# A tuned two-layer hybrid transformer trunk: the gated sum's halves in buffers of their own, copied one gate step behind each sum, and the second output tile's weights rounded earlier

## The chip, the cores and the metric

One core of one Trainium2 chip. The metric is the device time of one execution in microseconds; a kernel's time is the median of its runs. Durations of single instructions come from one further execution that was profiled.

## What is computed

The reference is a trunk of two layers over 512 latent and 256 context tokens of width 1024. Each layer normalises and modulates its input, projects it, and feeds three token mixers (grouped-query attention A, neighbourhood attention B, gated DeltaNet C). The change lies where the three are merged:

```python
def merge_branches(o_a, o_b, o_c, gate_raw, w_branch, w_out):
    br = jnp.einsum('btnc,ncd->btnd', jnp.stack([o_a, o_b, o_c], axis=-2), w_branch)
    gates = jax.nn.sigmoid(heads(gate_raw, N_BRANCH))
    return jnp.sum(gates * br, axis=-2) @ w_out
...
    x = x + gt_m * merge_branches(o_a, o_b, o_c, gate, w_branch, w_out)
    x = x + gt_f * sq_relu_mlp(modulate(rms_norm(x, norm_ffn), sh_f, sc_f), w_ffn1, w_ffn2)
```

All of it is float32. Layer 0 works on 768 tokens (context and latent), layer 1 from here on only on the 512 latent ones.

## The kernel before

Activations are kept transposed: partitions are channels, a *slice* `k` is 128 of the 1024 channels by all tokens. Each projection multiplies in three passes to keep float32 accuracy: the weights and the activations are each split into a high part, rounded to the type `fp32r`, and a low part, the rest. `project` (L452) adds high x high, high x low and low x high (L461, L462, L463) over the eight slices, and the 768 tokens go in two runs of 496 and 272 columns. `project_abreast` (L466) does the same for several output tiles, five slices of all tiles first, then the other slices tile by tile, with a wait (`ready`) for each slice, so that it can begin before all slices are there; its matmuls are L475, L476, L477.

The weights come tile by tile in one fixed order (`order`). SP brings a tile into one of three places of `wring`; ACT rounds it into `wh` (`high`, L1135, one of three places, free when TensorE has finished the tile three before); POOL subtracts and writes `wl` (`split`, L1903). TensorE waits for POOL's part (`weights`). `high(l, name, i)` rounds up to two tiles beyond the one named, `ahead=0` only as far as that one. Each engine's instructions stand in program order, and an engine that waits holds all that stands behind.

The stage around the change, for each layer:

- TensorE computes, for x = 0 to 23, the gate tile x (from the normalised input, halves `hh` and `hl`) and the branch tile x (from a branch's halves `ohi`, `olo`). x runs over branch C, then A, then B, with eight output slices each. Then the eight output tiles follow, 0 and 1 abreast, from the halves of the gated sum.
- ACT takes the sigmoid of gate tile x (L1368). DVE multiplies it with branch tile x (L1808) and, from x = 8, adds it to the sum `mT` (L1811). The sum's slice k is complete at x = 16 + k.
- The sum's halves go into `hh` (ACT, L1375) and `hl` (DVE, L1796), the buffers from which the gate projections read. So they wait for gate projection 23. ACT copies the eight slices there, and only behind them rounds the weights of output tiles 1 and 2. On DVE the first subtraction stands before the last multiplication, the other seven behind the last addition.
- Behind the output tiles ACT squares the new residual for the norm (L1072), TensorE sums the squares, and ACT and DVE make the new `hh` and `hl`.

`R` is one buffer of 27648 words for each partition that the stages share: the branch outputs and their halves, the sum `mT` at 9216 (`S0`), the sigmoids `gsig` at 15360, the norm's squares `sq_n`, root `rs_n` and products `ht`, and the feed-forward temporaries `ftmp`.

Of the kernel before, what the change touches and what calls it, by code (L numbers as in the profile page):

```python
# [15 lines left out]
F32 = mybir.dt.float32  # L16
F32R = mybir.dt.float32r
ALU = mybir.AluOpType
ACT = mybir.ActivationFunctionType
AX = mybir.AxisListType  # L20

P = 128
D = 1024
KC = D // P
LAT, CTX = 512, 256
TOK = LAT + CTX
# [16 lines left out]
GF = 4  # L43
# [65 lines left out]
def program(nc, a, out, x_store, skew, bias_rows, z_store, book):  # L109
    book["final"] = book.get("final", False)  # L110
    with ExitStack() as ctx:
# [28 lines left out]
        hh, hl = (ctx.enter_context(nc.sbuf_tensor(n, [P, KC, TOK], F32R)) for n in ("hh", "hl"))  # L140
# [9 lines left out]
        r_at = nc.sbuf_base if not callable(nc.sbuf_base) else nc.sbuf_base()  # L150
        r_at = (r_at + 31) // 32 * 32
# [11 lines left out]
        def r(at, *shape):  # L163
            n = int(np.prod(shape))
            v = R[:, at:at + n]
            if len(shape) == 2:
                v = v.rearrange("p (a b) -> p a b", a=shape[0])
            if len(shape) == 3:
                v = v.rearrange("p (a b c) -> p a b c", a=shape[0], b=shape[1])
            return v  # L170
# [2 lines left out]
        oC, oA, oB = r(0, 4, TOK), r(3072, 4, TOK), r(6144, 4, TOK)  # L173
        S0 = 9216

        N0 = 4 * GF * TOK
        sq_n, rs_n, ht = r(N0, 2, TOK), r(N0 + 2 * TOK, TOK), r(N0 + 3 * TOK, 3, TOK)
        ftmp = r(N0, 2, TOK)
        xT = r(XT0, KC, TOK)
        fin_T = nc.alloc_sbuf_tensor_at("fin_T", [P, KC, LAT], F32, offset=h_at)  # L180

# [31 lines left out]
        eraw = r(S0 + 3072, 2, 8, 32)  # L213

        mT = r(S0, KC, TOK)
        gsig = r(S0 + 6144, 2, TOK)
        prow = sb("prow", [P, P])
        mrow = sb("mrow", [P, P])
# [48 lines left out]
        act_done, dve_done, pool_done, pe_done = sig("act_done"), sig("dve_done"), sig("pool_done"), sig("pe_done")  # L267
# [14 lines left out]
        def full(*key):  # L282
            n = book.get(("ps",) + key, 0) if book["final"] else 0
            return ps_full[n % 4], n // 4 + 1
# [36 lines left out]
        def att_pairs(l):  # L321

            return [(br, hp, t) for br in "AB" for hp in range(A_H // 2) for t in range(TT if l == 0 else LT)]
# [109 lines left out]
        def weights(pe, l, name, i=0):  # L433

            pe.wait_ge(*pool_done.at("wlo", l, name, i))
            s = where[l, name, i][2] % NSPL
            return slot_view(wh, s, l, name, i), slot_view(wl, s, l, name, i)
# [10 lines left out]
        def _(pe):  # L448
            turn["n"] = 0
            mm, tr = nc.tensor.matmul, nc.tensor.transpose  # L450

            def project(key, w, ntok, rhs=None, kn=KC, m0=0, ready=None, ps=None, done=True):  # L452

                (ah, al), (rh, rl) = w, rhs or (hh, hl)
                ps = take(pe, *key)[:, landing(ntok):landing(ntok) + ntok]
                for t0, t1 in runs(ntok):
                    for k in range(kn):
                        if ready and t0 == 0:
                            pe.wait_ge(*ready(k))
                        ahk, alk = ah[:, k, m0:m0 + P], al[:, k, m0:m0 + P]  # L460
                        mm(ps[:, t0:t1], ahk, rh[:, k, t0:t1], start=(k == 0), stop=False)  # L461
                        mm(ps[:, t0:t1], ahk, rl[:, k, t0:t1], start=False, stop=False)  # L462
                        last = mm(ps[:, t0:t1], alk, rh[:, k, t0:t1], start=False, stop=(k == kn - 1))  # L463
                last.then_inc(*filled(*key))

            def project_abreast(jobs, ntok, ready):  # L466

                homes = [take(pe, *key)[:, landing(ntok):landing(ntok) + ntok] for key, _ in jobs]

                def products(i, k):  # L470

                    key, (ah, al) = jobs[i]
                    for t0, t1 in runs(ntok):
                        to = homes[i][:, t0:t1]
                        mm(to, ah[:, k, :], hh[:, k, t0:t1], start=(k == 0), stop=False)  # L475
                        mm(to, ah[:, k, :], hl[:, k, t0:t1], start=False, stop=False)  # L476
                        last = mm(to, al[:, k, :], hh[:, k, t0:t1], start=False, stop=(k == KC - 1))  # L477
                    return last

                for k in range(ABREAST):  # L480
                    pe.wait_ge(*ready(k))
                    for i in range(len(jobs)):
                        products(i, k)
                for i, (key, _) in enumerate(jobs):
                    for k in range(ABREAST, KC):
                        if i == 0:
                            pe.wait_ge(*ready(k))
                        last = products(i, k)
                    last.then_inc(*filled(*key))
# [199 lines left out]
            for l in range(DEPTH):  # L689
                if l == 0:  # L690

                    for t in range(TT):
                        pe.wait_ge(*x_in[t].at())
                        ps = take(pe, "x", t)
                        for k in range(KC):
                            last = tr(ps[:, k * P:k * P + P], r(S0 + 1024 * t, 1024)[:, k * P:k * P + P], ident)
                        last.then_inc(*filled("x", t))
                if l == 0:
# [8 lines left out]
                    for t in range(TT):  # L707
                        last = mm(ps[:, t * P:t * P + P], small[:, 16 + t:17 + t].to_broadcast([P, P]), ident,
                                  start=True, stop=True)
# [15 lines left out]
                for p in range(2, 15):  # L725
# [9 lines left out]
                    if p == 2:  # L735
                        pe.wait_ge(*read("baT", l))
                        ps = take(pe, "ba", l)
                        for t in range(TT):
                            last = tr(ps[:, 16 * t:16 * t + 16], baT[0:16, t * P:t * P + P], ident[0:16, 0:16])
                        last.then_inc(*filled("ba", l))  # L740
                    if p == 6:
# [7 lines left out]
                        for c in range(2):  # L749
                            last = mm(sums[:, :, 16 + 8 * c:24 + 8 * c], blk[:, 64 * c:64 * c + 1].to_broadcast([P, P]),  # L750
                                      gt[:, :, :], start=True, stop=True)
# [21 lines left out]
                for s in range(TT):  # L773
                    turned = None
                    for i in range(5):
                        for d in range(2):
# [3 lines left out]
                            last = halves(ps, srcT, src)  # L780
                            if i < 4:
                                last = halves(ps[:, 512:768], src, srcT)
# [16 lines left out]
                    for d in range(2):  # L799
# [3 lines left out]
                        for h in range(C_H):  # L803
                            for c, lo in enumerate((0, HALF)):
                                c0 = 512 * c + h * HALF
                                last = mm(ps[:, c0:c0 + HALF], kbuf[d][lo:lo + HALF, h, :], xbuf[d][lo:lo + HALF, h, :],  # L806
                                          start=True, stop=True)
# [5 lines left out]
                    for c in range(2):  # L813
                        n = 2 * s + c
# [8 lines left out]
                        for h in range(C_H):  # L823
                            for d in range(2):
                                mm(new[d][:, h * P:h * P + P], xbuf[d][rows[d], h, :], vbbuf[d][rows[d], h, :],
                                   start=(h == 0), stop=False)
# [4 lines left out]
                        for h in range(C_H):  # L831
                            for d in range(2):
                                ins = mm(new[d][:, h * P:h * P + P], cdbuf[d][:, chunk[d], h, :], S[:, 4 * d + h, :],
                                         start=False, stop=(h == C_H - 1))
# [3 lines left out]
                        o = [so[d][rows[d], 512:1024] for d in range(2)]  # L838
                        if out_wanted:
# [3 lines left out]
                            for h in range(C_H):  # L843
                                for d in range(2):
                                    mm(o[d][:, h * P:h * P + P], qdbuf[s % 2][d][:, chunk[d], h, :], S[:, 4 * d + h, :],
                                       start=(h == 0), stop=False)
# [60 lines left out]
                for x in range(24):  # L907
# [4 lines left out]
                            ready=(lambda k: dve_done.at("olo", l, n, k)) if x % 8 == 0 else None)  # L912
                    slot_read(l, "br", x, "br", l, x)
                project_abreast([(("out", l, i), weights(pe, l, "out", i)) for i in range(2)], nt,
                                lambda k: dve_done.at("mlo", l, k))
                for i in range(8):
                    if i >= 2:
                        project(("out", l, i), weights(pe, l, "out", i), nt)
                    slot_read(l, "out", i, "out", l, i)

                if l == DEPTH - 1:
# [142 lines left out]
        def _(act):  # L1064
            A = nc.scalar.activation
# [87 lines left out]
            for l in range(DEPTH):  # L1153
# [202 lines left out]
                def branch_high(l, n, k):  # L1356

                    A(ohi[n][:, k, 0:nt], (oA, oB, oC)[n][:, k, 0:nt], ACT.Copy).then_inc(*act_done.mark("ohi", l, n, k))

                act.wait_ge(*dve_done.at("o", l, len(att_pairs(l)) - 1))  # L1360
                for k in range(4):
                    branch_high(l, 2, k)
                for x in range(24):
# [4 lines left out]
                    A(gsig[:, x % 2, 0:nt], landed(nt, "gate", l, x), ACT.Sigmoid).then_inc(*free("gate", l, x))  # L1368
                    if 1 <= x < 9:
                        branch_high(l, (x - 1) // 4, (x - 1) % 4)  # L1370
                for k in range(KC):

                    act.wait_ge(*full("gate", l, 23))
                    act.wait_ge(*dve_done.at("merge", l, 16 + k))
                    A(hh[:, k, 0:nt], mT[:, k, 0:nt], ACT.Copy).then_inc(*act_done.mark("mhi", l, k))  # L1375
                for i in range(8):
                    high(l, "out", i)
                    if i == 0:
# [43 lines left out]
        def _(dve):  # L1422
# [128 lines left out]
            for l in range(DEPTH):  # L1551
# [241 lines left out]
                def merged_low(l, k):  # L1793

                    dve.wait_ge(*act_done.at("mhi", l, k))
                    V.tensor_tensor(hl[:, k, 0:nt], mT[:, k, 0:nt], hh[:, k, 0:nt].bitcast(F32), ALU.subtract)\  # L1796
                        .then_inc(*dve_done.mark("mlo", l, k))

                for x in range(24):
                    n, dc = divmod(x, 8)  # L1800
                    if x == 23:

                        dve.wait_ge(*full("gate", l, 23))
                        merged_low(l, 0)
                    dve.wait_ge(*full("br", l, x))
                    dve.wait_ge(*read("gate", l, x))
                    g, acc = gsig[:, x % 2, 0:nt], mT[:, dc, 0:nt]
                    V.tensor_tensor(g if n else acc, landed(nt, "br", l, x), g, ALU.mult).then_inc(*free("br", l, x))  # L1808
                    dve.wait_ge(*read("br", l, x))
                    if n:  # L1810
                        V.tensor_tensor(acc, acc, g, ALU.add).then_inc(*dve_done.mark("merge", l, x))  # L1811
                    else:
                        V.memset(small[:, 63:64], 0.0).then_inc(*dve_done.mark("merge", l, x))
                    if 1 <= x < 9:
                        branch_low(l, (x - 1) // 4, (x - 1) % 4)
                for k in range(1, KC):
                    merged_low(l, k)

                def residual(key, j, gate):

# [325 lines left out]
```

## Time and profile before

| | us |
|---|---|
| median of 3 runs | 3033.19 |
| lowest, highest | 3032.58, 3040.96 |
| the profiled execution, its own time | 3049.55 |
| its span | 3047.8 |
| TensorE matmuls busy (PE) | 2868.9 (94%) |
| TensorE weight loads busy (PEld) | 2456.4 (81%) |
| DVE busy | 1182.2 (39%) |
| ACT busy | 1034.4 (34%) |
| POOL busy | 1032.9 (34%) |
| granted TensorE clock, mean | 0.982 |

Busy times are sums over an engine's instructions in the one profiled execution; PE and PEld are the same engine, whose weight loads run beside its matmuls. Matmuls are pipelined: one is listed with 0.39 us, and the next starts 0.22 us later. The stage of the change is at 1155 to 1186 us in layer 0 and at 2622 to 2645 us in layer 1.

### The profile page before, as it was taken

The page shows a single profiled execution, that of the slowest core. Times are in us where ns is not written, and L with a number is a line of the kernel's source. Part 1 is how long each engine was busy: PE and PEld are TensorE (multiplying, and loading weights), DVE is VectorE, ACT ScalarE, POOL GpSimd, SP SyncE. Part 2 cuts the span into 40 slices and gives each one's busy share as a digit, 9 for nine tenths or more (in the row PEclk, how much of TensorE's full clock was granted, in tenths as well). Part 3 has the DMA queues.
Part 4 walks back from the last instruction along what each step waited for, and adds up shares of the span by engine and source line. Part 5 has one row for each costly group of instructions (what it writes and reads, how often), then busy time and mean ns, then how long its engine had stood idle before and what let it go on. Part 6 is the DMA issues. An engine that isn't in the chain of part 4 may idle for free. (4 is left out here: it accounts for less than half of the span.)

```text
span 3047.8 us, 57451 instructions
## 1 busy us (share of the span) xinstructions
PE 2868.9 (94%) x24823; PEld 2456.4 (81%) x24823; DVE 1182.2 (39%) x1813; ACT 1034.4 (34%) x1763; POOL 1032.9 (34%) x697
## 2 busy tenths in 40 slices
PE   6998899998999999999999999899999999999999
PEld 5887788876688888788888878788786788778887
DVE  3754443245631113422222267555235711242223
ACT  3542222225532112422222245433226532342223
POOL 3334434220323333222222223355430344434443
PEclk8999999999999999999999999999999999999999
DMA  7226344110012232122222122100320034323332
GB/s 252 63 67 214 136 150 132 42 42 1 12 42 64 64 108 63 49 63 63 64 69 63 63 83 63 43 3 3 90 56 2 15 100 135 95 83 96 97 101 80
DMA packets 306028, 230.89 MB, mean 76 GB/s; under 512 B 25265, under 2 KB 277617, under 8 KB 304881
## 3 DMA queue, kind: packets, MB, share of 16 engines
q1 hardware_dynamic: 299152, 202.48, 22.1%
q0 software_dynamic: 3776, 17.91, 1.6%
q10 hardware_dynamic: 2848, 6.82, 0.6%
q8 instruction: 198, 3.24, 0.4%
q14 instruction: 54, 0.43, 0.0%
HBM read 216.17 MB, written 11.98 MB: 75 GB/s over the span
## 5 line engine op out<-in xcount | busy, mean ns | idle before, releaser
L1903 POOL TENSOR_TENSOR wl<-wring,wh 128x1024 fp32r<-128x1024 f32 (+1 forms) x310 | 721.3, 2328 | 1358.7 <-ACT wh L1135 1354.3
L461 PE MATMUL ps<-hh,wh 128*128 128x496 f32 (+2 forms) x2312 | 822.8, 356 | 6.5 <-DVE R L1754 3.5
L463 PE MATMUL ps<-hh,wl 128*128 128x496 f32 (+2 forms) x2312 | 811.4, 351 | 0.0
L462 PE MATMUL ps<-hl,wh 128*128 128x496 f32 (+2 forms) x2312 | 811.1, 351 | 0.0
L461 PEld LDWEIGHTS ps<-hh,wh 128*128 128x128 f32 x2312 | 436.4, 189 | 69.5 <-issue 6.6
L462 PEld LDWEIGHTS ps<-hl,wh 128*128 128x128 f32 x2312 | 436.8, 189 | 57.3 <-issue 3.6
L463 PEld LDWEIGHTS ps<-hh,wl 128*128 128x128 f32 x2312 | 436.2, 189 | 54.6
L1135 ACT ACTIVATE wh<-wring 128x1024 fp32r<-128x1024 f32 (+1 forms) x310 | 305.7, 987 | 498.6 <-PE ps L463 458.9
L1824 DVE SCALAR_TENSOR_TENSOR R<-ps,modcs,R 128x512 f32<-128x512 f32 x216 | 136.3, 659 | 362.6 <-PE ps L463 339.8
L461 PE MATMUL ps<-fh,wh 128*128 128x496 f32 (+2 forms) x768 | 272.6, 355 | 0.0
L463 PE MATMUL ps<-fh,wl 128*128 128x496 f32 (+2 forms) x768 | 272.0, 354 | 0.0
L462 PE MATMUL ps<-fl,wh 128*128 128x496 f32 (+2 forms) x768 | 271.6, 354 | 0.0
L617 PE MATMUL ps<-R 64*64 64x64 f32 x5376 | 181.9, 221 | 27.9 <-issue 8.5
L617 PEld LDWEIGHTS ps<-R 64*64 64x64 f32 x5376 | 167.6, 136 | 44.2 <-issue 22.7
L1843 DVE TENSOR_TENSOR R<-R 128x768 f32<-128x768 f32 (+1 forms) x64 | 66.1, 1032 | 341.1 <-ACT R L1392 341.1
L1808 DVE TENSOR_TENSOR R<-ps,R 128x768 f32<-128x768 f32 (+1 forms) x48 | 39.6, 824 | 392.7 <-PE ps L463 392.7
L462 PEld LDWEIGHTS ps<-fl,wh 128*128 128x128 f32 x768 | 144.7, 188 | 19.0
L463 PEld LDWEIGHTS ps<-fh,wl 128*128 128x128 f32 x768 | 144.4, 188 | 19.4
L461 PEld LDWEIGHTS ps<-fh,wh 128*128 128x128 f32 x768 | 144.4, 188 | 19.2
L990 ACT ACTIVATE R<-ps,stat 128x768 f32<-128x768 f32 (+2 forms) x160 | 116.4, 730 | 119.6 <-DVE stat L1496 117.1
L1496 DVE TENSOR_REDUCE stat<-ps 128x1 f32<-128x768 f32 (+2 forms) x160 | 114.5, 741 | 38.0 <-PE ps L571 35.8
L1392 ACT ACTIVATE R<-ps 128x768 f32<-128x768 f32 (+1 forms) x64 | 45.1, 705 | 235.7 <-PE ps L463 174.2
(257 smaller groups left out, 3873.8 us busy)
## 6 DMA issues: line engine op xcount, KB each, us to landing
wring<-in_w_ffn SPq DMA_DIRECT2D x128, 512.0 KB, 3.6
wring<-in_w_in SPq DMA_DIRECT2D x110, 512.0 KB, 3.6
wboth<-in_w_mod SPq DMA_DIRECT2D x80, 512.0 KB, 6.3
wring<-in_w_branch SPq DMA_DIRECT2D x32, 256.0 KB, 2.7
wring<-in_w_out SPq DMA_DIRECT2D x16, 512.0 KB, 4.1
x_store<-R POOLq DMA_DIRECT2D x2, 3072.0 KB, 9.9
R<-x_store POOLq DMA_DIRECT2D x2, 3072.0 KB, 10.9
wring<-in_w_in SPq DMA_DIRECT2D x16, 256.0 KB, 3.4
```

The costliest lines, as they stand in the source:

```text
L461: mm(ps[:, t0:t1], ahk, rh[:, k, t0:t1], start=(k == 0), stop=False)
L462: mm(ps[:, t0:t1], ahk, rl[:, k, t0:t1], start=False, stop=False)
L463: last = mm(ps[:, t0:t1], alk, rh[:, k, t0:t1], start=False, stop=(k == kn - 1))
L617: last = mm(out[lo:lo + HALF, h * HALF:h * HALF + HALF], left[lo:lo + HALF, h, :], right[lo:lo + HALF, h, :], start=True, stop=True)
L990: nc.scalar.activation(prob[br][p % 2][:, u, 0:n], score_ps(l, p)[u][:, 0:n], ACT.Exp, bias=stat[:, sl, 0:1], accum_out=stat[:, sl, 1:2])\
L1135: A(slot_view(wh, n % NSPL, *slot), w, ACT.Copy).then_inc(*act_done.mark("whi", *slot))
L1392: A(f, landed(nt, "ff1", l, j), ACT.Relu).then_inc(*free("ff1", l, j))
L1496: V.tensor_reduce(stat[:, sl, 0:1], ps[:, 0:n], AX.X, ALU.max, negate=True)\
L1808: V.tensor_tensor(g if n else acc, landed(nt, "br", l, x), g, ALU.mult).then_inc(*free("br", l, x))
L1824: V.scalar_tensor_tensor(out=xT[:, j, t0:t1], in0=landed(nt, *key)[:, t0:t1], scalar=modc[:, gate + j, c:c + 1], in1=xT[:, j, t0:t1], op0= ...
L1843: V.tensor_tensor(f, f, f, ALU.mult).then_inc(*dve_done.mark("fsq", l, j))
L1903: G.tensor_tensor(slot_view(wl, n % NSPL, l, name, i), w, slot_view(wh, n % NSPL, l, name, i).bitcast(F32), ALU.subtract)\
```

## The change

1. The gated sum's halves are `mh`, at word 0 of `R` (over the branch buffers that are used up by then), and `ml`, in the place of `mT` itself. Output projections read them (`rhs=(mh, ml)`).
2. ACT copies slice k at gate step x = 17 + k, behind that step's sigmoid, and slice 7 behind the loop; the wait for gate projection 23 is gone. DVE subtracts slice k at the start of step 17 + k, before that step's multiplication, and slice 7 behind the loop.
3. At x = 23 ACT rounds output tile 1's weights directly behind the sigmoid, before it copies slices 6 and 7.
4. Since `ml` now stays in use during the output projections, the norm's squares, root and products get other places in `R` (`rs_n` at 15360, `sq_n` at 16896, `ht` behind it); `ftmp` stays at 12288.

```diff
-        N0 = 4 * GF * TOK
-        sq_n, rs_n, ht = r(N0, 2, TOK), r(N0 + 2 * TOK, TOK), r(N0 + 3 * TOK, 3, TOK)
-        ftmp = r(N0, 2, TOK)
+        N0 = 16896
+        rs_n, sq_n, ht = r(15360, TOK), r(N0, 2, TOK), r(N0 + 2 * TOK, 3, TOK)
+        ftmp = r(4 * GF * TOK, 2, TOK)
...
+        mh, ml = (nc.alloc_sbuf_tensor_at(n, [P, KC, TOK], F32R, offset=r_at + 4 * o) for n, o in (("mh", 0), ("ml", S0)))
...
-            def project_abreast(jobs, ntok, ready):
+            def project_abreast(jobs, ntok, ready, rhs=None):
+
+                rh, rl = rhs or (hh, hl)
...
                 project_abreast([(("out", l, i), weights(pe, l, "out", i)) for i in range(2)], nt,
-                                lambda k: dve_done.at("mlo", l, k))
+                                lambda k: dve_done.at("mlo", l, k), rhs=(mh, ml))
                 for i in range(8):
                     if i >= 2:
-                        project(("out", l, i), weights(pe, l, "out", i), nt)
+                        project(("out", l, i), weights(pe, l, "out", i), nt, rhs=(mh, ml))
...
+                def merged_high(l, k):
+
+                    act.wait_ge(*dve_done.at("merge", l, 16 + k))
+                    A(mh[:, k, 0:nt], mT[:, k, 0:nt], ACT.Copy).then_inc(*act_done.mark("mhi", l, k))
...
-                for k in range(KC):
-
-                    act.wait_ge(*full("gate", l, 23))
-                    act.wait_ge(*dve_done.at("merge", l, 16 + k))
-                    A(hh[:, k, 0:nt], mT[:, k, 0:nt], ACT.Copy).then_inc(*act_done.mark("mhi", l, k))
+                    if x == 23:
+                        high(l, "out", 1, ahead=0)
+                    if x >= 17:
+                        merged_high(l, x - 17)
+                merged_high(l, KC - 1)
...
-                    V.tensor_tensor(hl[:, k, 0:nt], mT[:, k, 0:nt], hh[:, k, 0:nt].bitcast(F32), ALU.subtract)\
+                    V.tensor_tensor(ml[:, k, 0:nt], mT[:, k, 0:nt], mh[:, k, 0:nt].bitcast(F32), ALU.subtract)\
...
-                    if x == 23:
-
-                        dve.wait_ge(*full("gate", l, 23))
-                        merged_low(l, 0)
+                    if x >= 17:
+                        merged_low(l, x - 17)
...
-                for k in range(1, KC):
-                    merged_low(l, k)
+                merged_low(l, KC - 1)
```

The order of ACT's instructions from the sigmoid of step 22 to the rounding of output tile 2, layer 0, before (`wh` is rounded weights, 128x512 a branch tile's, 128x1024 the others'; the square of the new residual follows later):

```order
L1368 ACTIVATE R<-ps 128x768
L1135 ACTIVATE wh<-wring 128x512
L1135 ACTIVATE wh<-wring 128x1024
L1368 ACTIVATE R<-ps 128x768
L1375 ACTIVATE hh<-R 128x768 x8
L1135 ACTIVATE wh<-wring 128x1024 x2
L1077 ACT_TABLE_LOAD
```

and in the changed kernel:

```order
L1377 ACTIVATE R<-ps 128x768
L1367 ACTIVATE mh<-R 128x768
L1139 ACTIVATE wh<-wring 128x512
L1139 ACTIVATE wh<-wring 128x1024
L1377 ACTIVATE R<-ps 128x768
L1139 ACTIVATE wh<-wring 128x1024
L1367 ACTIVATE mh<-R 128x768 x2
L1139 ACTIVATE wh<-wring 128x1024
L1081 ACT_TABLE_LOAD
```

Each list begins with the sigmoid of step 22. Tile 1's weights now stand directly behind the sigmoid of step 23 and before the last two copies; the other six copies are spread over the steps before.

DVE's instructions over steps 22 and 23 and the last halves, layer 0, before:

```order
L1808 TENSOR_TENSOR R<-ps,R 128x768
L1811 TENSOR_TENSOR R<-R 128x768
L1796 TENSOR_TENSOR hl<-R,hh 128x768
L1808 TENSOR_TENSOR R<-ps,R 128x768
L1811 TENSOR_TENSOR R<-R 128x768
L1796 TENSOR_TENSOR hl<-R,hh 128x768 x7
```

and in the changed kernel:

```order
L1805 TENSOR_TENSOR ml<-R,mh 128x768
L1815 TENSOR_TENSOR R<-ps,R 128x768
L1818 TENSOR_TENSOR R<-R 128x768
L1805 TENSOR_TENSOR ml<-R,mh 128x768
L1815 TENSOR_TENSOR R<-ps,R 128x768
L1818 TENSOR_TENSOR R<-R 128x768
L1805 TENSOR_TENSOR ml<-R,mh 128x768
```

One subtraction now precedes each multiplication, and one instead of seven stands behind the last addition.

## Rows read from the trace of the kernel before

**Rows 1.** The page, part 1: busy us, share of the span, instructions.
```profile
PE 2868.9 (94%) x24823; PEld 2456.4 (81%) x24823; DVE 1182.2 (39%) x1813; ACT 1034.4 (34%) x1763; POOL 1032.9 (34%) x697
```

**Rows 2.** Timeline, layer 0: start, us, engine, line, operation, count [idle before <-releaser].
```profile
1155.24 0.81 ACT L1368 ACTIVATE R<-ps 128x768 f32<-128x768 f32 x1 [7.26 <-PE ps L463]
1155.95 5.23 ACT L1375 ACTIVATE hh<-R 128x768 fp32r<-128x768 f32 x7
...
1159.05 0.29 PE L463 MATMUL ps<-ohi,wl 128*128 128x272 f32 x1
...
1160.43 0.96 DVE L1811 TENSOR_TENSOR R<-R 128x768 f32<-128x768 f32 x1
...
1162.23 1.99 ACT L1135 ACTIVATE wh<-wring 128x1024 fp32r<-128x1024 f32 x2
...
1163.41 2.78 POOL L1903 TENSOR_TENSOR wl<-wring,wh 128x1024 fp32r<-128x1024 f32 x1 [12.28 <-ACT wh L1135]
...
1166.29 0.75 PE L475 MATMUL ps<-hh,wh 128*128 128x496 f32 x1 [6.95 <-POOL wl L1903]
```

**Rows 3.** Timeline, layer 1.
```profile
2622.16 0.60 ACT L1368 ACTIVATE R<-ps 128x512 f32<-128x512 f32 x1 [4.37 <-PE ps L463]
...
2622.65 4.37 ACT L1375 ACTIVATE hh<-R 128x512 fp32r<-128x512 f32 x8
...
2624.40 0.39 PE L463 MATMUL ps<-ohi,wl 128*128 128x512 f32 x1
...
2626.93 1.99 ACT L1135 ACTIVATE wh<-wring 128x1024 fp32r<-128x1024 f32 x2
...
2628.11 2.80 POOL L1903 TENSOR_TENSOR wl<-wring,wh 128x1024 fp32r<-128x1024 f32 x1 [7.71 <-ACT wh L1135]
...
2631.01 0.76 PE L475 MATMUL ps<-hh,wh 128*128 128x512 f32 x1 [6.22 <-POOL wl L1903]
```

**Rows 4.** Timeline: one slice apart near the end of tile 1, both layers.
```profile
1184.91 0.39 PE L475 MATMUL ps<-hh,wh 128*128 128x496 f32 x1
...
1185.97 0.39 PE L461 MATMUL ps<-hh,wh 128*128 128x496 f32 x1
...
2643.92 0.39 PE L475 MATMUL ps<-hh,wh 128*128 128x512 f32 x1
...
2644.60 0.39 PE L461 MATMUL ps<-hh,wh 128*128 128x512 f32 x1
```

**Rows 5.** Timeline of POOL and DVE; last, the subtraction's min/median/max ns.
```profile
1147.90 0.96 DVE L1811 TENSOR_TENSOR R<-R 128x768 f32<-128x768 f32 x1
1148.12 3.00 POOL L1903 TENSOR_TENSOR wl<-wring,wh 128x1024 fp32r<-128x1024 f32 x1 [2.63 <-ACT wh L1135]
...
1184.26 2.41 POOL L1903 TENSOR_TENSOR wl<-wring,wh 128x1024 fp32r<-128x1024 f32 x1 [15.02 <-ACT wh L1135]
...
2617.93 2.47 POOL L1903 TENSOR_TENSOR wl<-wring,wh 128x1024 fp32r<-128x1024 f32 x1 [1.39 <-ACT wh L1135]
...
L1796 DVE TENSOR_TENSOR hl<-R,hh x16: 678/948/3129, 1156.9 to 2634.2; 128x768 fp32r<-128x768 f32 x8, 128x512 fp32r<-128x512 f32 x8
```

**Rows 6.** Timeline: TensorE's starts after two shorter idle times.
```profile
334.15 1.04 PE L617 MATMUL ps<-R 64*64 64x64 f32 x29 [2.03 <-issue]
...
700.91 1.87 PE L571 MATMUL ps<-R 64*128 64x512 f32 x4 [1.57 <-ACT R L990]
```

**Rows 7.** Windows: A:B us, busy of PE, PEld, DVE, ACT, POOL; granted clock, DMA, GB/s.
```profile
334.20:338.00 3.80, 3.75 (x114) 3.42 (x117) 1.77 (x5) 0.77 (x2) 0.00 (x0) 1.00 0.90 336
...
700.90:704.60 3.70, 3.69 (x18) 2.03 (x20) 1.54 (x4) 0.41 (x2) 0.00 (x0) 0.54 0.00 0
...
1240.50:1250.70 10.20, 6.39 (x22) 5.31 (x23) 8.06 (x14) 6.32 (x10) 0.82 (x1) 0.50 0.19 53
...
2631.00:2636.40 5.40, 5.39 (x13) 4.24 (x14) 3.84 (x3) 0.00 (x0) 2.69 (x1) 0.50 0.60 175
...
2680.90:2687.70 6.80, 3.99 (x15) 3.15 (x16) 5.22 (x9) 3.71 (x6) 1.46 (x1) 0.50 0.27 77
```

More of the change, by code:

```diff
@@ L474, in products @@
                         to = homes[i][:, t0:t1]
-                        mm(to, ah[:, k, :], hh[:, k, t0:t1], start=(k == 0), stop=False)
-                        mm(to, ah[:, k, :], hl[:, k, t0:t1], start=False, stop=False)
-                        last = mm(to, al[:, k, :], hh[:, k, t0:t1], start=False, stop=(k == KC - 1))
+                        mm(to, ah[:, k, :], rh[:, k, t0:t1], start=(k == 0), stop=False)
+                        mm(to, ah[:, k, :], rl[:, k, t0:t1], start=False, stop=False)
+                        last = mm(to, al[:, k, :], rh[:, k, t0:t1], start=False, stop=(k == KC - 1))
                     return last
```

## The prediction, made blind

> **What bounds the kernel now.** I read the page first. TensorE is busy for 2868.9 us, 94% of the span [rows 1], so work that is shifted on the other engines pays only where TensorE stands still for it. The change touches one place in each of the two layers, so the second view is the timeline around the step from the last branch projection to the first output tiles. In layer 0 the last branch matmul starts at 1159.05 and ends at 1159.34; the next one starts at 1166.29 after 6.95 us of idle time, released by POOL's low half of the weights [rows 2]. In layer 1 the end is 2624.79 (2624.40 and 0.39), the next start 2631.01, the idle time 6.22 us, the releaser the same [rows 3]. Those 13.17 us are what is there to be had directly.
>
> Follow the chain back in layer 0. Output tiles 0 and 1 are computed abreast, so TensorE waits for the weights of both. POOL splits the weights of tile 1 from 1163.41, because ACT rounded them at 1162.23, because ACT first copied eight slices of the gated sum: seven from 1155.95 to 1161.18, and the eighth behind the last addition, which DVE ended at 1161.39. ACT had been free for something else since the sigmoid of 1155.24. Layer 1 reads the same: eight copies from 2622.65, the rounding at 2626.93, POOL at 2628.11.
>
> A third view, the windows, gives the second cost. TensorE's granted clock is 0.50 (1.2 GHz, half of 2.4) from 2631.00 to 2636.40, while the matmuls start again [rows 7]; in layer 0 it is likewise. Its price is read from start to start. At full clock one slice of one tile takes 1.06 us in layer 0 (1184.91 to 1185.97) and 0.68 us in layer 1 (2643.92 to 2644.60) [rows 4]; 16 of them are 16.88 us (16 x 1.055, the second decimal being rounded in the rows) and 10.88 us. They took 1185.97 - 1166.29 = 19.68 us and 2644.60 - 2631.01 = 13.59 us. The low clock after the idle time costs 2.80 + 2.71 = 5.51 us.
>
> **The change part by part.**
>
> *The high halves move.* Eight ACT copies per layer no longer write the buffer that the gate projections read, so they need not wait for gate projection 23. Slice k is copied at gate step 17 + k, behind the sigmoid; the eighth stays at the end. Nothing is added: the same eight copies, of some 0.75 us (5.23 / 7) in layer 0 and 0.55 us (4.37 / 8) in layer 1. What is queued behind a copy on ACT are the roundings for the next branch and gate tiles. Their lows are ready early: the one that TensorE needs at the end of layer 1's branch 23 (2624.79) is done at 2617.93 + 2.47 = 2620.40 [rows 5], 4.4 us before; in layer 0 it is 1151.12 for 1159.34, 8.2 us before. That cover pays for a copy, so I cost it at nothing.
>
> *The low halves move.* Eight DVE subtractions (0.95 and 0.68 us, [rows 5]) go ahead of the multiplication of the same step. DVE waits there for the copy, some 1.6 us after a gate projection ends, while the branch result comes 4.1 us after it in layer 0 (1155.24 to 1159.34) and 2.6 in layer 1. 1.6 + 0.95 and 1.2 + 0.68 fit. Nothing, again.
>
> *Tile 1's weights are rounded ahead.* The rounding now sits directly behind the last sigmoid, where the first copy started: 1155.95 and 2622.65. From ACT's start to POOL's start it was 1162.23 to 1163.41 and 2626.93 to 2628.11, 1.18 to 1.20 us both times. POOL therefore starts at about 1157.15 and 2623.84. The length of POOL's instruction is the one open term. The same shape took 2.78 and 2.80 us in these two places, 2.41 us at 1184.26, 2.47 us at 2617.93, and 3.00 us at 1148.12, where DVE's addition (1147.90 to 1148.86) was under way when it started [rows 5]. At 1157.15 and 2623.84 no DVE instruction is under way, so I take 2.41 and 2.45, with 3.00 as the other end. The low half of slice 6 on DVE then starts while POOL works. Subtractions beside POOL took up to 3.129 us where the median was 0.948 [rows 5]; it is stretched to about POOL's end, and pushes the last multiplication, addition, copy and subtraction by 1 to 2 us. The last of them, low half 7, is then ready at about 1164.5 and 2630, and TensorE asks for it only after ten abreast products and two more (12 x 1.055 and 12 x 0.68 us): at 1172.3 and 2634.5. This is hidden.
>
> Here the Trainium skill has a rule that speaks against the edit. The page "SBUF — State Buffer", section "SBUF: two separate sides", says that GpSimd and a VectorE instruction with two SBUF inputs share a port pair as an exclusive lock, so that the one which starts first holds it and the other blocks. If a subtraction got in first, POOL would stand for up to a whole subtraction, and the sum below would be smaller by up to 0.95 + 0.68 us. By the order of starts above POOL is first, and then the rule and my sum agree.
>
> TensorE's first matmul came 0.10 us after POOL's end both times (1163.41 + 2.78 to 1166.29, 2628.11 + 2.80 to 2631.01). The new starts are 1157.15 + 2.41 + 0.1 = 1159.66 and 2623.84 + 2.45 + 0.1 = 2626.39. Gained: 1166.29 - 1159.66 = 6.63 us and 2631.01 - 2626.39 = 4.62 us, together 11.25. Idle time of 0.3 and 1.6 us is left; the weights of tile 1 are late still, and they remain the releaser.
>
> *The clock.* After 2.03 us of idle time before 334.15 the granted clock stayed at 1.00; after 1.57 us before 700.91 it was 0.54 [rows 6, 7]. With 0.3 us in layer 0 I expect no fall; with 1.6 us in layer 1 either is possible. Matmuls run without a break on both sides of it, so I take no fall, and 5.51 us come back whole. A fall would cost at most the old 2.71.
>
> *The homes of the norm's squares, roots and products move.* No instruction, shape or wait changes with them; zero, and the first use of the new places is behind the last read of the old contents. No row of the trace shows an address costing time: the branch halves in the same buffer and the halves in the old one both give matmuls of 0.39 us.
>
> **Sum.** 11.25 + 5.51 = 16.8 us. Against the profiled execution's 3049.55 that is 3032.8. The median of the runs shown is 3033.19, 16.36 us below that execution; none of the terms depends on the difference, so I subtract there too: **3016.4 us**, 0.55% faster. Changes within 0.3% (9.1 us) could hardly be told from none here; the runs shown lie 8.4 us apart.
>
> **Rivals.**
>
> *A, the forecast.* Both gaps nearly close and the clock holds: 3016.4. Bounds of its terms: both POOL instructions at 3.00 us give 3017.5; no idle time left at all gives 3014.5. Chance 0.68.
>
> *B, the clock falls in layer 1 after all.* 2.7 us come back as loss, with POOL's 1.1 us: 3020.2. For it: 0.54 after 1.57 us. Against it: 1.00 after 2.03 us. Chance 0.14.
>
> *C, the gain is given back in later clock stretches.* Everything behind 1160 moves, and how long the clock stays low after a stall differs between like stalls. The norm of layer 0 had 10.2 us at 0.50 and the same norm in layer 1 6.8 us [rows 7]; the 3.4 us between them cost 1.7 us of work. Some ten stalls follow the first saved place; if five of them get a longer stretch, 8.5 us go: 3024.9, which is no longer to be told from no change. Against it: as many should get shorter. Chance 0.15.
>
> *D, slower.* The halves in the gate steps hold up the weights of the next tiles, in 14 steps (17 to 23, two layers). Price: each step adds its copy and subtraction to TensorE's path, 7 x (0.75 + 0.95) + 7 x (0.55 + 0.68) = 20.5 us, and the clock drops each time for 3.4 us, 14 x 1.7 = 23.8 us. 3016.4 + 44.3 = 3060.7. It decides from the point where the lows of a next tile come over 4.4 us later than now in layer 1, or 8.2 in layer 0. A copy and a locked subtraction beside it together are 3.7 us at most. Chance 0.03.
>
> **How the numbers follow.** The likeliest case gives 3016.4. A, B and C set the range: on the lower side A's 3014.5 less two or three clock stretches of luck, 3010; on the upper side up to just beyond C's middle, 3026. Over 9.1 us faster (below 3024.1): A, B and half of C, 0.88 rounded; within: the rest of C, 0.09; slower by over 9.1 us: D, 0.03.
>
> **What would show it.** Right: in the timeline the rounding of tile 1's weights directly behind the last sigmoid; POOL's split of 2.4 us; TensorE's idle time before the first output product at 0.3 and 1.6 us instead of 6.95 and 6.22, with the same releaser; granted clock 1.00 there; no idle time of TensorE in gate steps 17 to 23; one slow low half beside POOL. Wrong: another releaser (a low half, the copy of slice 7) before the first or the thirteenth product; a clock of 0.50 behind 2626; idle time before a gate or branch product; or a span that falls by much less than these two places gained, with longer stretches at 0.50 elsewhere.

## The result and the profile after

| | median, us | lowest to highest | runs |
|---|---|---|---|
| before, measured beside the change | 3037.19 | 3032.58 to 3044.78 | 6 |
| the change | 3022.05 | 3013.66 to 3027.44 | 6 |

The ratio is 0.9946, with a 95% interval of 0.9928 to 0.9965: 16.4 us less, between 10.6 and 21.9. (The ratio is worked out from all the runs and is not the quotient of the two medians, which lie 15.1 us apart.) Measured again beside the experiments, with another eight runs of the changed kernel, it was 0.9959 (0.9941 to 0.9978), 12.5 us less. The forecast was 16.8 us, 0.55%. One execution of an experiment below, of the kernel with the early rounding alone, took 10638.85 us at a granted clock of 0.481, and its ratio leaves it out.

The page of the changed kernel, its header and the line of part 1:

```profile
span 3020.4 us, 57433 instructions
...
PE 2855.1 (95%) x24823; PEld 2451.2 (81%) x24823; DVE 1180.0 (39%) x1813; ACT 1033.6 (34%) x1763; POOL 1032.0 (34%) x697
```

The instruction counts are those of before [rows 1], and the busy times of DVE, ACT and POOL agree with it within 2.2 us. The timeline of layer 0, for comparison with [rows 2] (this execution is 2.04 us ahead of the other at this place, for reasons that lie before it):

```profile
1153.20 0.81 ACT L1377 ACTIVATE R<-ps 128x768 f32<-128x768 f32 x1 [7.26 <-PE ps L465]
1153.91 1.05 ACT L1139 ACTIVATE wh<-wring 128x1024 fp32r<-128x1024 f32 x1
1154.86 0.84 ACT L1367 ACTIVATE mh<-R 128x768 fp32r<-128x768 f32 x1
1155.10 2.39 POOL L1909 TENSOR_TENSOR wl<-wring,wh 128x1024 fp32r<-128x1024 f32 x1 [6.02 <-ACT wh L1139]
1155.72 2.58 DVE L1805 TENSOR_TENSOR ml<-R,mh 128x768 fp32r<-128x768 f32 x1 [8.91 <-ACT mh L1367]
...
1157.01 0.29 PE L465 MATMUL ps<-ohi,wl 128*128 128x272 f32 x1
1157.59 0.46 PE L479 MATMUL ps<-mh,wh 128*128 128x496 f32 x1 [0.30 <-POOL wl L1909]
...
1159.21 0.96 DVE L1818 TENSOR_TENSOR R<-R 128x768 f32<-128x768 f32 x1
1160.20 0.85 ACT L1367 ACTIVATE mh<-R 128x768 fp32r<-128x768 f32 x1 [4.51 <-DVE R L1818]
...
1161.08 0.96 DVE L1805 TENSOR_TENSOR ml<-R,mh 128x768 fp32r<-128x768 f32 x1 [0.91 <-ACT mh L1367]
```

and of layer 1, for [rows 3]:

```profile
2601.93 1.05 ACT L1139 ACTIVATE wh<-wring 128x1024 fp32r<-128x1024 f32 x1
2602.88 0.62 ACT L1367 ACTIVATE mh<-R 128x512 fp32r<-128x512 f32 x1
2603.12 2.36 POOL L1909 TENSOR_TENSOR wl<-wring,wh 128x1024 fp32r<-128x1024 f32 x1 [3.44 <-ACT wh L1139]
2603.53 2.50 DVE L1805 TENSOR_TENSOR ml<-R,mh 128x512 fp32r<-128x512 f32 x1 [6.11 <-ACT mh L1367]
...
2605.58 0.47 PE L479 MATMUL ps<-mh,wh 128*128 128x512 f32 x1 [1.51 <-POOL wl L1909]
```

The rounding (L1139) stands directly behind the sigmoid (L1377), POOL's split (L1909) takes 2.39 and 2.36 us, and TensorE's idle time is 0.30 and 1.51 us with POOL's weights as its releaser still. The low half of slice 6 (L1805), which starts while POOL works, is stretched to 2.58 and 2.50 us; the last low half is done at 1162.04, and nothing on TensorE waits for it.

The windows of the changed kernel, first the gate steps 17 to 23 of both layers up to the last branch matmul (in layer 0 from 5.5 us behind the start of step 17), then the abreast products (columns as in [rows 7]):

```profile
1075.00:1157.20 82.20, 82.20 (x481) 73.92 (x479) 18.71 (x19) 21.27 (x27) 29.19 (x14) 1.00 0.33 106
2545.00:2603.90 58.90, 58.90 (x261) 48.59 (x259) 15.21 (x21) 19.75 (x29) 28.08 (x16) 1.00 0.49 156
...
1157.30:1172.00 14.70, 14.41 (x81) 12.86 (x82) 4.08 (x5) 3.58 (x5) 2.59 (x2) 1.00 0.25 72
2605.20:2616.00 10.80, 10.42 (x46) 8.69 (x47) 3.57 (x5) 4.30 (x6) 2.71 (x3) 1.00 0.33 99
```

TensorE is busy for the whole of the gate steps, and its trace shows no idle time before any matmul of them, so the halves cost nothing there. The granted clock behind the two places is 1.00. Before, it was 0.50 in layer 1 [rows 7] and likewise in layer 0:

```profile
1166.30:1172.10 5.80, 5.80 (x18) 5.09 (x19) 5.49 (x4) 0.00 (x0) 2.94 (x1) 0.50 0.57 167
```

**A measure that does not depend on the rest of the execution.** From the start of the last branch matmul to the start of output tile 2's first matmul the work is the same in every kernel here. Before, it ran from 1159.05 to 1185.97 and from 2624.40 to 2644.60 [rows 2 to 4]: 26.92 + 20.20 = 47.12 us. In the changed kernel it runs from 1157.01 to 1174.62 and from 2603.68 to 2616.55: 17.61 + 12.87 = 30.48 us. The two places give 16.64 us. Below, this sum is *the two places*.

The spans differ by more, 3047.8 - 3020.4 = 27.4 us. Of the other 10.8 us, 2.04 had come before 900 us, where both kernels do the same, and 6.6 us came in layer 0's feed-forward stage, which the last section takes up. The rest, some 2 us, is 0.3 us between the first place and that stage and 2.5 us between it and the second place, less 0.7 us lost behind the second place; the last section shows that such stretches differ from execution to execution.

### The profile page after: what moved, and what is told of

Read it like the earlier page. It is cut to its first block and busy times, and to the rows that moved or that the text cites. A ratio compares the mean times of both kernels' runs of the same rounds, so it can differ in the third digit from the quotient of the medians.

```text
span 3020.4 us, 57433 instructions
## 1 busy us (share of the span) xinstructions
PE 2855.1 (95%) x24823; PEld 2451.2 (81%) x24823; DVE 1180.0 (39%) x1813; ACT 1033.6 (34%) x1763; POOL 1032.0 (34%) x697
## 5 line engine op out<-in xcount | busy, mean ns | idle before, releaser
L1909 POOL TENSOR_TENSOR wl<-wring,wh 128x1024 fp32r<-128x1024 f32 (+1 forms) x310 | 720.7, 2326 | 1334.7 <-ACT wh L1139 1330.2
L463 PE MATMUL ps<-hh,wh 128*128 128x496 f32 (+2 forms) x2168 | 770.1, 355 | 6.5 <-DVE R L1763 3.5
L465 PE MATMUL ps<-hh,wl 128*128 128x496 f32 (+2 forms) x2168 | 759.5, 350 | 0.0
L464 PE MATMUL ps<-hl,wh 128*128 128x496 f32 (+2 forms) x2168 | 759.3, 350 | 0.0
L1139 ACT ACTIVATE wh<-wring 128x1024 fp32r<-128x1024 f32 (+1 forms) x310 | 305.8, 987 | 470.6 <-PE ps L465 448.1
L463 PEld LDWEIGHTS ps<-hh,wh 128*128 128x128 f32 x2168 | 408.9, 189 | 65.0 <-issue 6.6
L464 PEld LDWEIGHTS ps<-hl,wh 128*128 128x128 f32 x2168 | 409.3, 189 | 53.0 <-issue 3.4
L465 PEld LDWEIGHTS ps<-hh,wl 128*128 128x128 f32 x2168 | 408.8, 189 | 50.2
```

The costliest lines, as they stand in the source:

```text
L1139: A(slot_view(wh, n % NSPL, *slot), w, ACT.Copy).then_inc(*act_done.mark("whi", *slot))
L1909: G.tensor_tensor(slot_view(wl, n % NSPL, l, name, i), w, slot_view(wh, n % NSPL, l, name, i).bitcast(F32), ALU.subtract)\
```

## The experiments

Times are medians; each ratio is against runs of the kernel before on the same chip. The kernel before had 3043.35 us beside the first four kernels below, and 3041.17 us beside the other four.

### The early rounding alone

To the kernel before:

```diff
                     if 1 <= x < 9:
                         branch_high(l, (x - 1) // 4, (x - 1) % 4)
+                    if x == 23:
+                        high(l, "out", 1, ahead=0)
                 for k in range(KC):
```

> The kernel before, with one edit: output tile 1's weights are rounded directly behind the sigmoid of step 23; the halves stay in the old buffers and at their old places. My theory: both parts are needed, and this one alone closes most of layer 0's gap and part of layer 1's. POOL's split then starts at about 1157.2 and 2623.8 as in the changed kernel, but the low halves come late: the first one is stretched beside POOL, the second stands behind the last multiplication and addition. Idle time of TensorE from the last branch matmul to the fourth slice: about 1.8 us in layer 0 (6.95 before), about 4 us in layer 1 (6.22 before), in pieces before several slices, with DVE's low half as the releaser of the later pieces. Time: 10 to 13 us less than before. The rival, that the weights are all there is to it (the halves' new home is ornament): 16 to 17 us less, idle time 0.1 and 1.5 us. The other rival, that the halves set the start: 1 us less or none.

Measured: 3033.9 us, ratio 0.9967 (0.9951 to 0.9982), 10.0 us less. The two places: 19.07 (1152.48 to 1171.56) + 14.00 us = 33.07 us, 14.05 less than before. The timeline of this kernel, layer 0, then the two starts of layer 1:

```profile
1149.44 1.05 ACT L1135 ACTIVATE wh<-wring 128x1024 fp32r<-128x1024 f32 x1
1150.39 5.24 ACT L1377 ACTIVATE hh<-R 128x768 fp32r<-128x768 f32 x7
1150.64 2.39 POOL L1905 TENSOR_TENSOR wl<-wring,wh 128x1024 fp32r<-128x1024 f32 x1 [5.93 <-ACT wh L1135]
1151.33 2.52 DVE L1798 TENSOR_TENSOR hl<-R,hh 128x768 fp32r<-128x768 f32 x1 [8.88 <-ACT hh L1377]
...
1153.99 0.46 PE L475 MATMUL ps<-hh,wh 128*128 128x496 f32 x1 [1.22 <-DVE hl L1798]
...
1156.63 0.49 PE L475 MATMUL ps<-hh,wh 128*128 128x496 f32 x1 [0.29 <-DVE hl L1798]
...
2603.66 0.47 PE L475 MATMUL ps<-hh,wh 128*128 128x512 f32 x1 [2.13 <-DVE hl L1798]
2605.50 0.50 PE L475 MATMUL ps<-hh,wh 128*128 128x512 f32 x1 [0.21 <-DVE hl L1798]
```

The releaser changed, as expected: TensorE now waits for the first low half, which is held up beside POOL, and shortly for the second. But these waits are 1.5 and 2.3 us, not 1.8 and about 4. In layer 1 I had reckoned with one more locked subtraction in the way of slices 2 and 3. The trace has POOL's next split only at 2606.67, 1.17 us behind the start of the second slice, and no idle time of TensorE behind it. One line gives 84% of what the whole change gives at the two places.

### The halves' move alone

From the changed kernel:

```diff
-                    if x == 23:
-                        high(l, "out", 1, ahead=0)
```

> The changed kernel without the early rounding of output tile 1's weights: the halves have their own home and are made one step behind each sum, the weights are rounded where they were, behind the copy of slice 7. My theory: next to nothing. The copy of slice 7 waits for the last addition, the rounding comes behind it at its old time, POOL starts at its old time and only takes 2.4 instead of 2.8 us: idle time 6.6 and 5.8 us, low clock afterwards as before, time 1 us less than before. The rival, that the eight copies were the cause: 10 us or more less.

Measured: 3038.85 us, ratio 0.9989 (0.9973 to 1.0005), which can't be told from 1. The two places: 24.98 + 19.85 = 44.83 us, 2.29 less. The timeline of this kernel:

```profile
1160.38 0.96 DVE L1816 TENSOR_TENSOR R<-R 128x768 f32<-128x768 f32 x1
1161.37 0.84 ACT L1367 ACTIVATE mh<-R 128x768 fp32r<-128x768 f32 x1 [4.63 <-DVE R L1816]
1162.12 1.99 ACT L1139 ACTIVATE wh<-wring 128x1024 fp32r<-128x1024 f32 x2
...
1163.30 4.67 POOL L1907 TENSOR_TENSOR wl<-wring,wh 128x1024 fp32r<-128x1024 f32 x2 [12.22 <-ACT wh L1139]
...
1165.74 0.75 PE L479 MATMUL ps<-mh,wh 128*128 128x496 f32 x1 [6.45 <-POOL wl L1907]
...
2623.67 0.77 PE L479 MATMUL ps<-mh,wh 128*128 128x512 f32 x1 [5.71 <-POOL wl L1907]
```

Seven of eight copies were gone from the way, and the rounding started when it had before: the eighth copy waits for the last addition, and the rounding stands behind it. What is won is 0.50 and 0.51 us of idle time, since DVE is no longer in POOL's way (two splits in 4.67 us instead of 5.83 and 5.58), and some 1.4 us by a shorter low clock in layer 0, which only this one profile shows. The parts nearly add up: 14.05 and 2.29 us for 16.64. The halves' move is worth 2.3 us by itself, and 2.6 us behind the early rounding.

### The new places of the norm's data alone

The kernel before with only the lines on `N0`, `rs_n`, `sq_n`, `ht` and `ftmp` changed.

> The kernel before with only the norm's squares, root and products in their new places. My theory: no change (within 2 us), idle times 6.95 and 6.22 us as before. In the profiles of the two kernels layer 0's feed-forward stage had a pace of 220 ns from one 496-column matmul to the next in the changed kernel and 221 to 227 ns before, some 6.5 us over the stage. If the new places were the reason (the rival), this kernel's feed-forward stage has 220 ns and the time is 5 to 7 us less than before; if it is a matter of the single execution, the pace of this profile is one or the other and the time is unchanged.

Measured: 3041.73 us, ratio 0.9993 (0.9979 to 1.0008). Idle times 6.95 and 6.22 us, the two places 47.08 us: no change. Its profile did have the faster pace of the feed-forward stage, and yet its median stands with the kernel before, so the new places are not what makes the stage shorter. The next run and the last one tell the rest.

### The changed kernel once more

> The changed kernel once more, unaltered, for its spread and a second profile. Expected: 16 us less than before (13 to 19), idle time 0.1 us in layer 0 and 1.5 us in layer 1, granted clock 1.00 at both places. If the 220 ns pace of layer 0's feed-forward stage belongs to this kernel, it is there again; if to the single execution, it may be 221 to 227 ns.

Measured: 3030.37 us (3025.43 to 3036.59), ratio 0.9959 (0.9941 to 0.9978), idle times 0.36 and 1.52 us (0.1 and 1.5 expected), the two places 17.67 + 12.91 = 30.58 us. 12.5 us less than before is short of the 13 that I had set as the lower end; its interval, 6.7 to 18.0 us, holds the 16.6 of the two places. The pace of the feed-forward stage was the slower one this time.

### Weights held back: the price of idle time

From the changed kernel, with two copies as shown, and in a second kernel with four (`range(4)`):

```diff
                     if x == 23:
+                        for _ in range(2):
+                            A(ht[:, 2, 0:LAT], cst[:, C_COS:C_COS + LAT], ACT.Copy).then_inc(*act_done.mark("idle", l, _))
+                            act.wait_ge(*act_done.at("idle", l, _))
                         high(l, "out", 1, ahead=0)
```

> The changed kernel with output tile 1's weights held back: ACT makes two copies of 512 columns of the constants into an unused place before it rounds them. Output unchanged. What it asks is the price of TensorE's idle time here, and from where on the clock falls. Two copies, each waited for, are some 1.5 us: idle time about 1.8 us in layer 0 and 3.0 us in layer 1 (0.3 and 1.5 without). If idle time alone counts, the two places together take 3 us more than in the changed kernel; if the clock falls behind the longer one, 2 to 3 us more on top.

> The same with four copies: idle time about 3.3 us in layer 0 and 4.5 us in layer 1. Idle time alone: 6 us more than the changed kernel at the two places. With the low clock behind both, as it was behind 6.95 and 6.22 us, up to 5.4 us more on top, 11 us in all. If the clock stays up behind 3.3 us, the layer 0 place costs its idle time only.

Measured: with two copies 3024.36 us, ratio 0.9945 (0.9925 to 0.9966); with four 3035.36 us, ratio 0.9981 (0.9966 to 0.9995). By total time the kernel with two copies can't be told from the changed one (0.9946). Each copy added 0.65 to 0.66 us of idle time, less than my 0.75. The two places took 34.57 and 38.80 us, 4.1 and 8.3 us more than in the changed kernel, for 2.6 and 5.2 us more of idle time. Both lie between the expectation for idle time alone (3 and 6 us) and the one with the low clock on top. The first output matmul of each place, with two copies (two rows) and with four:

```profile
1154.69 0.47 PE L479 MATMUL ps<-mh,wh 128*128 128x496 f32 x1 [1.60 <-POOL wl L1912]
2611.71 0.47 PE L479 MATMUL ps<-mh,wh 128*128 128x512 f32 x1 [2.82 <-POOL wl L1912]
```

```profile
1163.46 0.75 PE L479 MATMUL ps<-mh,wh 128*128 128x496 f32 x1 [2.90 <-POOL wl L1912]
2623.01 0.47 PE L479 MATMUL ps<-mh,wh 128*128 128x512 f32 x1 [4.14 <-POOL wl L1912]
```

and the windows behind them, again with two copies and with four:

```profile
1154.80:1166.00 11.20, 11.20 (x64) 9.98 (x65) 3.39 (x4) 3.29 (x4) 2.39 (x1) 1.00 0.32 95
2611.80:2615.50 3.70, 3.70 (x10) 2.88 (x11) 2.34 (x4) 1.97 (x3) 0.26 (x1) 0.54 0.48 142
```

```profile
1163.50:1166.60 3.10, 3.10 (x9) 2.68 (x10) 2.50 (x3) 0.54 (x1) 0.00 (x0) 0.50 0.57 166
2623.00:2627.50 4.50, 4.49 (x13) 3.54 (x14) 2.44 (x4) 2.67 (x3) 0.96 (x1) 0.62 0.41 117
```

Behind 1.60 us of idle time the clock stays at 1.00; behind 2.82, 2.90 and 4.14 us it is low for a while. Call *the extra* of a stop what the place takes beyond the run without idle time (next section: 16.98 and 11.11 us) and beyond the idle time itself: 0.2 us behind 1.60 us (18.80 - 16.98 - 1.60), 1.8 us behind 2.82 and 2.90, 1.9 us behind 4.14, and 3.0 and 2.9 us behind the 6.95 and 6.22 us of the kernel before. In the kernel with the halves' move alone it was 1.6 us behind 6.45 and 3.0 behind 5.71, so behind a long stop the extra isn't fixed. Not all of it is the clock's: with the clock at 1.00 throughout it was 0.3 us at each place in the changed kernel (17.61 - 16.98 - 0.30 and 12.87 - 11.11 - 1.51), and 0.6 us at each with the rounding alone, where TensorE stops twice at each place.

### Tile 0's first slices without tile 1's weights

From the changed kernel, in `project_abreast`, with `lead=3` for the output tiles and tile 1's `weights` called there:

```diff
-                for k in range(ABREAST):
+                for k in range(lead):
+                    pe.wait_ge(*ready(k))
+                    products(0, k)
+                if lead:
+                    key, load = jobs[1]
+                    jobs[1] = (key, load())
+                    homes.append(take(pe, *key)[:, landing(ntok):landing(ntok) + ntok])
+                    for k in range(lead):
+                        products(1, k)
+                for k in range(lead, ABREAST):
```

> The changed kernel with TensorE waiting for tile 1's weights only after the first three slices of tile 0. Those take 2.0 us in layer 1 and 3.2 us in layer 0, longer than the idle time left (1.5 and 0.3 us); slices 1 and 2 are there since two gate steps. Expected: no idle time at the first place (under 0.1 us), the two places together 1.8 us shorter than in the changed kernel, which the total time will hardly show: 14 to 19 us less than before. The rival: the idle time moves to the first product of tile 1 or to the last slices, nothing gained.

Measured: 3023.39 us, ratio 0.9939 (0.9916 to 0.9961), 18.6 us less than before. The windows of this kernel, each place from the last branch matmul to tile 2:

```profile
1159.44:1176.42 16.98, 16.98 (x99) 15.21 (x98) 5.24 (x6) 5.19 (x6) 4.57 (x3) 1.00 0.21 63
2609.76:2620.86 11.10, 11.10 (x50) 9.20 (x49) 5.12 (x5) 4.65 (x6) 4.81 (x3) 1.00 0.32 94
```

TensorE never stops. The two places take 28.09 us, 2.4 less than in the changed kernel. By this measure it beats both kernels. By total time it beats the one before; whether it beats the changed one can't be said from these intervals.

### The kernel before once more

> The kernel before, unaltered, for a second profile. Expected: idle times 6.95 and 6.22 us again, the low clock behind both; the pace of layer 0's stages 220 or 224 ns, either of the two for each stage.

One profile and no ratio: 3049.95 us. Idle times 6.95 and 6.22 us, the two places 27.04 + 20.13 = 47.17 us. The feed-forward stage of layer 0, from the same matmul to the same matmul, as windows of TensorE alone (us, busy, granted clock, DMA share, GB/s): the kernel before, its second profile, the changed kernel and its second profile, in this order:

```profile
1280.32:1777.67 497.35, 497.35 (x2863) 1.00 0.22 65
```

```profile
1285.77:1776.54 490.77, 490.77 (x2863) 1.00 0.22 66
```

```profile
1268.66:1759.43 490.77, 490.77 (x2862) 1.00 0.22 66
```

```profile
1262.41:1759.75 497.34, 497.34 (x2862) 1.00 0.22 65
```

Both kernels have shown both durations. The difference of 6.6 us at this stage is the execution's, not the kernel's.

### All runs at the two places

| kernel | idle, layer 0 | idle, layer 1 | the two places, us | less than before | ratio of totals |
|---|---|---|---|---|---|
| before | 6.95 | 6.22 | 47.12 | | |
| homes only | 6.95 | 6.22 | 47.08 | 0.04 | 0.9993 |
| halves only | 6.45 | 5.71 | 44.83 | 2.29 | 0.9989 |
| changed, four copies in the way | 2.90 | 4.14 | 38.80 | 8.3 | 0.9981 |
| changed, two copies in the way | 1.60 | 2.82 | 34.57 | 12.6 | 0.9945 |
| rounding only | 1.51 | 2.34 | 33.07 | 14.05 | 0.9967 |
| changed | 0.30 | 1.51 | 30.48 | 16.64 | 0.9946, 0.9959 |
| changed, tile 0 first | 0 | 0 | 28.09 | 19.0 | 0.9939 |

## Why the prediction was right

*The chain of the wait.* The prediction named the rounding of tile 1's weights, held behind the copies, as what TensorE waits for. The experiments confirm the chain and refine it: the rounding alone gives 14.05 of 16.64 us. The prediction costed the two moved halves at nothing and gave no worth to them either. Their worth is 2.6 us: without them the first low half is the next thing late.

*The terms.* From start to start the wait fell by 6.66 us in layer 0 (1166.29 - 1159.05 against 1157.59 - 1157.01) and 4.71 us in layer 1, together 11.4 for 11.25 foreseen. The rest of 16.64, 5.3 us, came behind the restarts, where the clock no longer fell, for 5.51 foreseen. POOL's split took 2.39 and 2.36 us for 2.41 and 2.45. Idle times of 0.30 and 1.51 us stood at 0.3 and 1.6.

*The clock in layer 1.* It did not fall behind 1.51 us, nor behind 1.52 us in the second profile. That was the choice between A and B. The stops of 1.60 and 2.13 us that the experiments made at the two places stayed at 1.00 too. But the prediction's rows could not decide it, and the row against it, 0.54 after 1.57 us [rows 6, 7], is the nearer one in length. That stop stands in all ten profiles, 1.57 or 1.58 us long each time: the clock was low behind it in four (0.54: before, changed, changed again, four copies) and 1.00 in six. In the second profile of the kernel before:

```profile
706.30:710.00 3.70, 3.64 (x32) 2.61 (x32) 2.52 (x5) 1.49 (x6) 0.00 (x0) 1.00 0.01 2
```

The same kernel shows both behind the same stop, so its length alone does not decide. What does stays open, and that rival B did not come is in part luck as far as this case shows.

*The port.* The low half of slice 6 began 0.62 and 0.41 us behind POOL's split and took 2.58 and 2.50 us, while POOL took its shortest time. In the kernel with the halves' move alone no subtraction was under way beside the split, and both splits took 4.67 us in place of 5.83. The delayed low halves ended 0.81 and 0.55 us behind POOL's end, nearly their own length without POOL (0.96 and 0.69 us). The Trainium skill's page "SBUF — State Buffer", section "SBUF: two separate sides", says that GpSimd and a VectorE instruction with two inputs in the on-chip memory (SBUF) share a port pair as an exclusive lock: the one that starts first holds it for its whole instruction, and the other blocks. The trace agrees: POOL started first and took 2.39 and 2.36 us. Here the delay falls on the one with time to spare.

*The gate steps.* No idle time of TensorE in steps 17 to 23; rival D had no place to act.

*The level.* 3022.05 lies 5.7 us above the 3016.4 forecast. Of this, 4.0 us is the kernel before, which came out at 3037.19 with six runs for 3033.19 with three; the other 1.7 us is the difference of the medians, 15.1 us for 16.8. Taking the level from three runs was the weak step. That the ratio gives 16.4 us is closer than such totals can be trusted for: the repeat gave 12.5. The two places, 16.64 and 16.59 us (47.17 - 30.58), are the firmer test.

*Rival C.* The stretches behind the saved places do differ from execution to execution, but the profiles show no loss that follows the change. From the end of layer 0's feed-forward window to layer 1's last branch matmul it was 846.7 us in both profiles of the kernel before, 844.3 and 849.3 us in those of the changed one. (In the prediction's chances, A, B and half of C are 0.895, which it gives as 0.88.)

## What to carry to other kernels

Follow a wait back until an engine's order decides it, and move the one instruction on which the late thing hangs; here it was one rounding behind eight copies, worth 84% of the gain. Then look which thing is late next, since a move that hardly shows alone (halves only: 1.0 us of idle time, 2.3 us at the places and nothing to be told in the total) can be what the first one needs to be whole. Where effects are under 1%, compare a stretch of equal work in the profiles from start to start; it repeated to 0.1 us here, while whole executions of one kernel lay 8 to 22 us apart.

## What was unexpected of the hardware

**Two paces for the same matmuls.** In the ten profiles the feed-forward stage of layer 0 took either 497.3 us (before, changed again, halves only, four copies) or 490.8 to 490.9 us (the other six), with nothing between, no idle time, and the clock at 1.00. The gate steps of layer 0 show the same: from the first branch matmul to the last, 288.3 us (rounding only, homes only, changed again) or 292.0 us (the other seven). From one 496-column matmul to the next it is 220.0 ns in the faster pace and 223.8 ns in the slower. The two stages take either pace independently of each other, and a stage keeps the pace with which it begins. These are stages of layer 0, where a tile's columns go in runs of 496 and 272; layer 1's gate steps, with a single run of 512, took 190.2 us in all ten. What chooses between the paces stays open and was not tried. They are a part of the spread of the totals, up to 10 us. Another part lies in stretches with many stops: up to the first branch matmul of layer 0, where all kernels do the same, the ten profiles took 853.3 to 865.0 us from the first matmul, and between layer 0's feed-forward stage and layer 1's last branch matmul 842.7 to 851.4 us.

**What a stop costs beyond its idle time.** At the two places the clock did not fall behind idle time of up to 2.13 us, and the extra was 0.2 to 0.3 us for one stop; it was 1.8 to 1.9 us from 2.82 to 4.14 us, and 1.6 to 3.0 us from 5.71 to 6.95 us, with the clock low behind each. This is no rule for other places: behind one and the same stop of 1.57 us in an attention stage the clock fell in four of ten profiles.
